# Carrying the routing weight with the slot, adding the other experts' rows while the last expert runs, bringing the last expert's rows to their tokens by a 0/1 product, and spreading the last norm over three engines

## What is computed

```python
# two experts a token, with weights; combine is (token, expert)
weights = jax.nn.softmax(e_top, axis=-1) * g_prob
act = (jax.nn.silu(hg) * hu).astype(jnp.float32) * combine[:, :, None]
y = jnp.einsum('nef,efd->nd', act.astype(x.dtype), w_down)
x = x + gt2[:, None, :] * y
# the final norm
y = xf * lax.rsqrt(jnp.mean(jnp.square(xf), axis=-1, keepdims=True) + EPS)
y = y * gain * (1.0 + scale) + shift
```

## Time and profile before

| | us |
|---|---|
| median of 3 runs | 1399.41 |
| fastest and slowest run | 1393.77, 1399.50 |
| the profiled execution's own time | 1396.18 |
| its span, first to last instruction | 1394.2 |
| PE busy | 1239.2 (89%) |
| PE weight loads busy | 946.7 (68%) |
| DVE busy | 670.4 (48%) |
| ACT busy | 543.9 (39%) |
| POOL busy | 207.4 (15%) |

### The profile page before, as it was taken

How to read it: one execution, slowest core, us unless ns; L and a number is a source line. 1 busy time by engine, 2 the same in 40 slices (tenths; PEclk the granted TensorE clock), 3 DMA queues, 4 the chain that set the end, 5 groups by cost and what they waited for, 6 DMA issues and landing times. The chain is left out here.

```text
span 1394.2 us, 17845 instructions
## 1 busy us (share of the span) xinstructions
PE 1239.2 (89%) x7111; PEld 946.7 (68%) x7111; DVE 670.4 (48%) x900; ACT 543.9 (39%) x872; POOL 207.4 (15%) x237
## 2 busy tenths in 40 slices
PE   3799999999989999998779999999998999999920
PEld 0477876777678887887656566747766888777710
DVE  0516622221151214122466542255686898888846
ACT  2333212101273135214333333302546777777731
POOL 2401300010000010001200011100053222322210
PEclk8699998999999998998889999999999999999965
DMA  9412311244443453438479996821469999999831
GB/s 362 155 61 91 98 35 57 91 161 139 165 158 85 158 206 115 161 121 329 167 252 347 364 352 185 287 86 43 141 229 346 372 369 382 372 375 378 311 145 68
DMA packets 125193, 289.95 MB, mean 208 GB/s; under 512 B 10084, under 2 KB 10204, under 8 KB 120456
## 3 DMA queue, kind: packets, MB, share of 16 engines
q1 hardware_dynamic: 106280, 236.49, 48.0%
q0 software_dynamic: 18848, 52.53, 10.6%
HBM read 270.37 MB, written 26.18 MB: 213 GB/s over the span
## 5 line engine op out<-in xcount | busy, mean ns | idle before, releaser
L962 PE MATMUL psum<-part,part 128*128 128x512 f32 (+1 forms) x1088 | 445.1, 409 | 9.5 <-DVE part L2248 5.9
L963 PE MATMUL psum<-part,part 128*128 128x512 f32 (+1 forms) x1088 | 430.9, 396 | 0.0
L964 PE MATMUL psum<-part,part 128*128 128x512 f32 (+1 forms) x1088 | 430.7, 396 | 0.0
L962 PEld LDWEIGHTS psum<-part,part 128*128 128x128 f32 (+1 forms) x1088 | 228.3, 210 | 76.0 <-issue 24.5
L964 PEld LDWEIGHTS psum<-part,part 128*128 128x128 f32 (+1 forms) x1088 | 228.2, 210 | 40.5
L963 PEld LDWEIGHTS psum<-part,part 128*128 128x128 f32 (+1 forms) x1088 | 229.1, 211 | 35.8
L2248 DVE TENSOR_TENSOR part<-arena,part 128x2048 fp32r<-128x2048 f32 x96 | 218.0, 2290 | 43.3 <-ACT part L1699 41.9
L1803 DVE TENSOR_TENSOR part<-arena,part 128x2048 fp32r<-128x2048 f32 x42 | 96.3, 2299 | 252.5 <-PE psum L1002 228.8
L1699 ACT ACTIVATE part<-arena 128x2048 fp32r<-128x2048 f32 x94 | 178.8, 1919 | 55.8 <-DMA arena<-in_w_up_dram 28.1
L1474 ACT ACTIVATE arena<-psum 128x512 f32<-128x512 f32 (+4 forms) x142 | 77.9, 571 | 272.7 <-PE psum L964 208.9
L950 PE MATMUL psum<-cst,arena 128*128 128x128 f32 (+3 forms) x857 | 128.1, 293 | 61.7 <-DMA cst<-in_consts_dram 12.6
(11 more groups left out here) (271 smaller groups left out, 1073.5 us busy)
## 6 DMA issues: line engine op xcount, KB each, us to landing
arena<-in_w_in_dram SPq DMA_DIRECT2D x34, 1024.0 KB, 5.5
arena<-in_cache_kv_w_dram SPq DMA_DIRECT2D x16, 2048.0 KB, 11.3
arena<-in_w_gate_dram SPq DMA_DIRECT2D x32, 1024.0 KB, 9.7
arena<-in_w_up_dram SPq DMA_DIRECT2D x32, 1024.0 KB, 9.2
arena<-in_w_down_dram SPq DMA_DIRECT2D x32, 1024.0 KB, 10.2
arena<-in_w_ada_dram SPq DMA_DIRECT2D x24, 1024.0 KB, 7.5
arena<-in_cache_kv_w_dram SPq DMA_DIRECT2D x16, 1024.0 KB, 9.0
arena<-in_w_ada_final_dram SPq DMA_DIRECT2D x8, 1024.0 KB, 7.9
```

Source lines behind the costliest of these rows:

```text
L962: nc.tensor.matmul(out_, hi, w_hi, start=start, stop=False)
L963: nc.tensor.matmul(out_, hi, w_lo, start=False, stop=False)
L964: last_product[0] = nc.tensor.matmul(out_, lo, w_hi, start=False, stop=stop)
```

## The change

1. A slot has three words instead of two: token, place, and the weight as float32. DVE computes the weights before it signals `rows_done`, and writes them into the third word of `tok_u`.
2. ACT's `result` uses the third word of `dest_u` as scale, so it waits for `dest_in`, the landing of the places. The weighting after the loop goes away.
3. `yd` is filled with zeros early: a memset and nine transfers on POOL between the two groups of `add_shift`. POOL waits for them before the expert loop, and DVE before it reuses the memory of the zeros.
4. The last expert has no scatter. POOL loads its places, waits for the scatter of the expert before, and loads `yd` back into `yg`, which now lies in the places of weights that have been read. POOL adds the two rows of tiles 2 to 4, DVE those of tiles 0 and 1.
5. DVE builds `hot_last`, ones where a slot's token is the row's, from the last expert's tokens, and PE multiplies it with the last expert's rows (`y_last`, already multiplied by the gate, for the prompt; the plain rows for the sample tile). DVE adds these products from PSUM to `x1`.
6. In the final norm of tiles 0 to 2 ACT scales by the root and POOL adds the shift; DVE does tiles 3 and 4.

```diff
-        slots_d = dram("slots_d", (E_ALL * EROWS + CAP, 2), U32)
+        slots_d = dram("slots_d", (E_ALL * EROWS + CAP, 3), U32)
...
+            nc.gpsimd.memset(zeros, 0.0).then_inc(y_zero, 1)
+            pool.wait_ge(y_zero, 1)
+            for r in range(2 * TOK // P):
+                pool.dma_start(yd[r * P:(r + 1) * P, :], zeros).then_inc(y_zeroed, 16)
...
-            for par in range(2):
-                scatter((E_ALL - 2 + par) * EROWS + (rounds - 1) * CAP, rounds * PAIRS, par)
+            scatter((E_ALL - 2) * EROWS + (rounds - 1) * CAP, rounds * PAIRS, 0)
+            waited()
+            load_places((E_ALL - 1) * EROWS + (rounds - 1) * CAP, 1)
             pool.wait_ge(xg_in[0], rounds * (PAIRS * 16) + 16)
-            for par in range(2):
-                pool.wait_ge(y_out[par], rounds * (PAIRS * 16) + 16)
+            pool.wait_ge(y_out[0], rounds * (PAIRS * 16) + 16)
+            pool.wait_ge(y_out[1], rounds * (PAIRS * 16))
+            pool.wait_ge(gate_filled, rounds * E_ALL)
             waited()
...
+            for i in range(2, TILES):
+                n = ROWS[i]
+                pool.wait_ge(yg_in[i], 16)
+                nc.gpsimd.tensor_tensor(yg[0:n, i, 0, :], yg[0:n, i, 0, :], yg[0:n, i, 1, :], ALU.add).then_inc(y_sum, 1)
...
+                if i < 3:
+                    pool.wait_ge(y_scaled, i + 1)
+                    nc.gpsimd.tensor_tensor(x1[:, i, :], x1[:, i, :], mod[:, 0, 0, :], ALU.add).then_inc(y_shifted, 1)
...
+            for _ in range(2):
+                nc.tensor.matmul(psum[:, 7, :], ident, c_("dmask"), start=True, stop=True)
+            for i in range(TILES):
+                n = ROWS[i]
+                if i == 4:
+                    pe.wait_ge(x2_done, 1)
+                for c in range(2):
+                    if i == 0:
+                        pe.wait_ge(last_done, c + 1)
+                    y = y_last[:, c * CH:(c + 1) * CH] if i < 4 else yb[:, 1, c * CH:(c + 1) * CH]
+                    ins = nc.tensor.matmul(psum[0:n, LAST_BANKS[i][c], :], hot_last[:, i, 0:n], y, start=True, stop=True)
+                ins.then_inc(last_filled, 1)
...
             def result(par, done, after):
                 act.wait_ge(y_out[par], after * 16)
+                act.wait_ge(dest_in[par], after * 16)
                 for c, (filled, out_) in enumerate(((y0_filled, y0_out), (y1_filled, y1_out))):
                     act.wait_ge(filled, done + 1)
-                    nc.scalar.activation(yb[:, par, c * CH:(c + 1) * CH], psum[:, 5 + c, :], ACT.Copy).then_inc(out_, 1)
+                    nc.scalar.activation(yb[:, par, c * CH:(c + 1) * CH], psum[:, 5 + c, :], ACT.Copy,
+                                         scale=dest_w[:, par, :]).then_inc(out_, 1)
...
+            for i in range(TILES):
+                n = ROWS[i]
+                act.wait_ge(x2_done, i + 1)
                 if i:
+                    act.wait_ge(sq3, i)
+                nc.scalar.activation(junk_end[0:n, :], x1[0:n, i, :], ACT.Square, accum_out=ss[0:n, i:i + 1]).then_inc(sq3, 1)
+                act.wait_ge(var3, i + 1)
+                nc.scalar.activation(rs[0:n, i:i + 1], rs[0:n, i:i + 1], ACT.Sqrt).then_inc(sqrt3, 1)
+                if i < 3:
+                    act.wait_ge(rs_done, i + 1)
+                    nc.scalar.activation(x1[:, i, :], yg[:, i, 0, :], ACT.Copy, scale=rs[:, i:i + 1]).then_inc(y_scaled, 1)
...
+            def add_earlier(i):
+                n, s = ROWS[i], i // 4
+                y1, y2, x = yg[0:n, i, 0, :], yg[0:n, i, 1, :], x1[0:n, i, :]
+                if i < 2:
+                    dve.wait_ge(yg_in[i], 16)
+                    own(V.tensor_tensor(y1, y1, y2, ALU.add))
+                else:
+                    dve.wait_ge(y_sum, i - 1)
+                own(V.tensor_tensor(y1, y1, mod[0:n, 2, s, :], ALU.mult))
+                own(V.tensor_tensor(x, x, y1, ALU.add))
...
+            for i in range(2):
+                add_earlier(i)
+            for c, out_ in enumerate((y0_out, y1_out)):
+                cols = slice(c * CH, (c + 1) * CH)
+                dve.wait_ge(out_, rounds * (2 * PAIRS) + 1)
+                V.tensor_tensor(y_last[:, cols], yb[:, 1, cols], mod[:, 2, 0, cols], ALU.mult).then_inc(last_done, 1)
+            add_earlier(2)
+            for i in range(TILES):
+                add_last(i)
+                if i:
+                    last_norm(i - 1)
+                variance(i)
+                if i < 2:
+                    add_earlier(3 + i)
+            last_norm(TILES - 1)
```

More of the change, by code:

```diff
@@ L373, in expert_half @@
             return at(first, 4, CH), *parts(first + HALF, first, 4, CH)
-        yg = at(4 * SLOT, TILES, 2, D)
-        junk_end = at(4 * SLOT + TILES * 2 * D, D)
+        yg = at(0, TILES, 2, D)
+        junk_end = at(TILES * 2 * D, D)
+        hot_last = at(3 * SLOT, TILES, P)
+        y_last = at(3 * SLOT + D, D)
+        zeros = at(KEPT0 + D, D)
         sgubT, sgubTs = stat[:, 640:648], stat[:, 648:656]
@@ L895, in fetch, with load_places @@
                     ap=slot_u[:, par, 0:1], axis=0), bounds_check=TOK - 1, oob_is_err=False).then_inc(xg_in[par], 16)
+            def load_places(row, par):
+                pool.dma_start(dest_u[:, par, :], slots_d[bass.ds(row, CAP), :]).then_inc(dest_in[par], 16)
             def scatter(row, after, par):
-                pool.dma_start(dest_u[:, par, :], slots_d[bass.ds(row, CAP), :]).then_inc(dest_in[par], 16)
+                load_places(row, par)
                 pool.wait_ge(dest_in[par], after * 16)
@@ L2266, in _ @@
                 own(V.tensor_reduce(rowf[:, k, :], pick, AX.X, ALU.add))
+            dve.wait_ge(rt_exp, 2)
+            own(V.tensor_reduce(gp, eg, AX.X, ALU.add))
+            own(V.reciprocal(gp, gp))
+            own(V.tensor_scalar(w1, w2, 1.0, None, ALU.add))
+            own(V.reciprocal(w1, w1))
+            own(V.tensor_tensor(w1, w1, gp, ALU.mult))
+            own(V.tensor_copy(tok_w[:, 0, :], w1))
+            own(V.tensor_tensor(tok_w[:, 1, :], w2, w1, ALU.mult))
             V.tensor_copy(row_u, rowf).then_inc(rows_done, 1)
@@ L2322, in _ @@
             scale_gain(1)
-            def add_experts(i):
-                n, s = ROWS[i], i // 4
-                y1, y2 = yg[0:n, i, 0, :], yg[0:n, i, 1, :]
-                x = x1[0:n, i, :]
-                dve.wait_ge(y1_scaled, i + 1)
-                own(V.scalar_tensor_tensor(out=y1, in0=y2, scalar=w2[0:n, i:i + 1], in1=y1, op0=ALU.mult, op1=ALU.add))
-                own(V.tensor_tensor(y1, y1, mod[0:n, 2, s, :], ALU.mult))
-                V.tensor_tensor(x, x, y1, ALU.add).then_inc(x2_done, 1)
-                dve.wait_ge(x2_done, i + 1)
-                own(V.tensor_tensor(y1, x, mod[0:n, 1, s, :], ALU.mult))
+            own(V.tensor_copy(last_tok, slot_u[:, 1, 0:1]))
@@ new lines, in _ @@
+            for i in range(TILES):
+                ins = V.tensor_scalar(hot_last[:, i, :], c_("iota"), float(P * i), last_tok, ALU.add, ALU.is_equal)
+            own(ins)
+            def add_earlier(i):
+                n, s = ROWS[i], i // 4
+                y1, y2, x = yg[0:n, i, 0, :], yg[0:n, i, 1, :], x1[0:n, i, :]
+                if i < 2:
+                    dve.wait_ge(yg_in[i], 16)
+                    own(V.tensor_tensor(y1, y1, y2, ALU.add))
+                else:
+                    dve.wait_ge(y_sum, i - 1)
+                own(V.tensor_tensor(y1, y1, mod[0:n, 2, s, :], ALU.mult))
+                own(V.tensor_tensor(x, x, y1, ALU.add))
@@ new lines, in add_last @@
+            def add_last(i):
+                n, s = ROWS[i], i // 4
+                dve.wait_ge(last_filled, i + 1)
+                for c in range(2):
+                    cols = slice(c * CH, (c + 1) * CH)
+                    u, x, t = psum[0:n, LAST_BANKS[i][c], :], x1[0:n, i, cols], yg[0:n, i, 1, cols]
+                    if i == 4:
+                        own(V.tensor_tensor(t, u, mod[0:n, 2, 1, cols], ALU.mult))
+                    ins = V.tensor_tensor(x, x, u if i < 4 else t, ALU.add)
+                    if c == 0:
+                        own(ins)
+                ins.then_inc(x2_done, 1)
+                dve.wait_ge(x2_done, i + 1)
+                own(V.tensor_tensor(yg[0:n, i, 0, :], x1[0:n, i, :], mod[0:n, 1, s, :], ALU.mult))
@@ L2343, in _ @@
-            for i in range(TILES + 1):
-                if i < TILES:
-                    add_experts(i)
+                V.reciprocal(rs[0:n, i:i + 1], rs[0:n, i:i + 1]).then_inc(rs_done, 1)
+                if i >= 3:
+                    dve.wait_ge(rs_done, i + 1)
+                    V.scalar_tensor_tensor(out=x1[0:n, i, :], in0=yg[0:n, i, 0, :], scalar=rs[0:n, i:i + 1],
+                                           in1=mod[0:n, 0, s, :], op0=ALU.mult, op1=ALU.add).then_inc(y_done, 1)
+            for i in range(2):
+                add_earlier(i)
```

74 lines of the change are left out of this document (29 added, 45 removed).

## The result

| us | before | after |
|---|---|---|
| median, of 4 runs each | 1399.22 | 1415.75 |
| lowest and highest run | 1393.77, 1399.50 | 1412.51, 1416.90 |
| ratio of the times, with 95% interval | | 1.0125 (1.0098 to 1.0151) |
| profiled execution | 1396.18 | 1416.11 |
| its span | 1394.2 | 1414.4 |

Of the 20.4 us between the two last DVE ops, 17.6 are there at the end of expert 1's result. The positions in time tell the rest: +2.1 from end(1) to end(13), -1.2 over the last two experts, +1.9 in the tail.

The account below looks back on a forecast made before the run. In the expert loop PE was busy 18.00 of 18.00 us and DMA too, at 375 GB/s. Profiled 1396.18 + 19 (wait) + 5 (ring) + 1 (tail) = 1421.2, said as 1421; bounds 1405 to 1433, range 1404 to 1434.

Parts of the forecast that it names:

- D: The prediction's own forecast for the whole kernel: slower, 1405 to 1433 us, chance 0.65.
- The wait on ACT: Expert 0's result waits for its places, PE goes idle, expert 1's result ends later: +19.0 us (bounds +16 and +20).
- steps in series: From expert 0's result to expert 1's, token copies, weight parts, gate, transposes, down products and evictions follow one another: 20.2 us.
- The ring: POOL's loop of scatter, index load, gather and places now includes ACT: period 18.8 us, +5 (bounds 0 and +12).
- The last two experts: End of the expert loop: no fetch in front, down weights set the pace as before, 0 us.
- The tail: From last result to last DVE op: +45.5 us against +44.4, so +1 (bounds -7 and +5).
- The walk: Step-by-step account of DVE's work behind the last result, tile by tile, ending at +46 to +47 us.
- PE's products for tile 0 end before: In the tail, PE's products (0.9 us each after idle) are done before DVE needs them.
- What was free: Zeroing yd early under idle time (13 us if uncovered), moved weight computation (at worst 1.5), third slot word: 0.
- A: Rival at expert 0's result: the wait is hidden and the tail gains; 1389 to 1392 us, chance 0.07.
- B: Rival: the wait is there, but the loop makes the stall good and the tail gains 7; 1401 to 1405 us, chance 0.13.
- C: Rival: POOL's ring bounds at full price and POOL's additions come last in the tail; 1436 to 1445 us, chance 0.15.

Follow-up runs that it names:

- x1: Kernel before plus one line: ACT's result also waits for the landing of the places, nothing else of the change; 1413.50 us, ratio 1.0079.
- x2: Changed kernel with expert 0's places loaded ahead of the modulation loads and each next expert's ahead of the scatter; 1401.37 us, ratio 1.0008.
- x3: Changed kernel with the early additions of tiles 2 to 4 on DVE instead of POOL; 1412.75 us, ratio 1.0084.
- x4: Changed kernel with the last norm step of tiles 0 to 2 back on DVE, without ACT's copy and POOL's addition; 1412.22 us, ratio 1.0078.
- x6: x5 with the six loads of the final modulation (2.25 MB) moved behind the scatter of expert 14; 1397.99 us, ratio 1.0000 to the kernel before.
- x7: Kernel before with only the six final modulation loads (2.25 MB) moved behind the scatter of expert 14; 1390.92 us, ratio 0.9938.
- x5: Changed kernel with the edits of x2, x3 and x4 together; 1393.99 us, ratio 0.9974 to the kernel before.
- x8: x5 with an expert's result behind the token copies and first two high parts in ACT's order; 1394.65 us, ratio 0.9976 to the kernel before.
- x9: x8 with modulation loads split by need: gate behind expert 14's scatter, scale and shift behind yd tiles 1 and 2; 1384.45 us, ratio 0.9911 to before.

## Why the prediction was right, point by point

The forecast D held: 1421 was said, 1415.75 measured (profiled 1416.11), slower by more than the measurement's error. The change itself came out smaller than said: the terms add up to 25 us, and the profiled executions are 19.9 apart, the medians 16.5. The two largest terms were both too large.

1. **The wait on ACT** (+19, bounds 16 to 20). Right in mechanism and nearly in size. First result at 1076.7 for 1078, end(0) 1078.0 for 1079.1, PE idle to 1083.13 for 1083, end(1) 1097.9 for 1099.3. The steps in series took 19.9 us for 20.2. The term measured +17.6, of which 1.6 came with the entry into the expert part; the remaining 16.0 are at the low bound. x1 shows it by itself, x2 takes most of it away. The places landed faster than the 5.3 us of my choice: the first landing is some 4 us behind its issue at 1072.46, as DMA was running out of work (226 GB/s from 1072 to 1077, after 313 in the five us before), with the weights stopped by the same stall. The landings of L914 in the changed kernel:

```profile
DMA to landing us min/median/max: 3.5/6.1/7.2
```

2. **The ring** (+5). This is the term that was mis-sized: +2.1. Its signs came, with 11 of 13 results right behind their places, but the period was 18.54 and not 18.8. The scatter took 1.01 in nearly every turn and not 1.2, the gather 1.05 to 2.6 and not 2.4, the places 5.65 in the turn shown and not 6.2. In a ring each small term counts once a turn: 0.26 us too much, twelve times, is 3 us. I had taken durations from single turns. That the ring costs anything over the loop isn't shown: from end(1) to end(13) the kernels in which ACT waits for places in most turns take 221.1 (x1), 222.3 (x3), 222.5 (after) and 223.4 us (x4), those in which it waits once or twice or never 220.1 (x6), 220.4 (before), 220.7 (x7), 220.9 (x2) and 223.2 (x5).

3. **The last two experts** (0). They gave 1.2 us back: 35.33 us from end(13) to end(15) against 36.54. The cause of that wasn't tried; x1 to x7 lie between 35.4 and 36.9, so it may be chance.

4. **The tail** (+1, bounds -7 to +5). +1.9 in the one profile, +1.0 by the means of three tails each (45.5 and 44.5). The walk was right in its places: DVE at the first tile at -4.4, `y_last` done at +10.6 for +11.7, tile steps of 5.3, 8.9, 5.2, 5.2 and 7.8 us for 5.5, 9.3, 5.5, 5.5 and 7.9. Added up, the walk gave +46 to +47, and 46.3 came; the +45.5 that went into the sum was lower than the walk, for no reason that a row gives. One step failed inside it: "PE's products for tile 0 end before". The earlier trace rows counts records, and a product of this kind leaves two: L1286 makes 32 full products in the kernel before and has 64 records. The changed kernel's chain:

```profile
1365.72 3.79 PE psum L1491 x4
```

These four records are the two products of tile 0. After 9.03 us of idle they take 1.9 us each, not 0.9, and end 0.95 us too late for DVE. DVE also waits 2.25 us in each of three tiles for ACT's square, which stands behind its copy. x4 has these three waits no more, for three operations of 1.28 us on DVE; its wait for PE stays (0.89).

5. **What was free.** Zeroing `yd` was, as said. POOL's timeline of the changed kernel:

```profile
68.30 0.95 POOL L799 MEMSET arena<- 128x1024 f32 x1
69.54 4.77 POOL L802 DMA_DIRECT2D yd<-arena  x9 [0.30 <-POOL arena L799]
130.62 2.88 POOL L794 TENSOR_TENSOR arena<-arena 128x1024 f32<-128x1024 f32 x1 [56.31 <-DVE arena L1933]
```

56.31 us of idle are left behind it.

6. **The rivals.** A (the wait hidden) fell with the first line of ACT's timeline: the condition was places landed before 1063, and they landed near 1076.5. B (the stall made good) was wrong in both halves: end(15) - G is 16.9 longer, as much as end(1) - G (16.0), so nothing was made good, and of the tail's 7 us most (6.1) came only in x5, with POOL out of it. C (the ring at full price) didn't come: the period stayed at 18.54. The range's low end, 1404, was 8.5 us below the fastest run; the high end, 1434, would have needed gathers of 3.0 us each turn and a tail 5 us longer.

What stays open: why the loops of x2, x5 and x8 are 5 to 6 us longer than before's although the places now come before the scatter. Part of it may be the fast execution of before, since x2's ratio is only 1.0008. The late first result (end(0) - G is 32.3 in x2 and x5, 27.2 before) isn't enough as a cause: x6 has it too (32.7), and with the modulation loads moved its loop is 307.8; x8 has no wait for places on ACT and still takes 314.2. So the runs point at the modulation loads, which x2, x5 and x8 also start some 4 us later than before. x9 changes ACT's order and the loads at once, so their shares aren't told apart.

## What to carry to other kernels

When a value travels with a table that an engine didn't have to read before, look up in the trace when that table lands now, and lay it beside the time at which its new reader wants it: a slack of a whole stage on a side engine costs nothing until something in the middle waits for it. Ask what stands ahead of the small load in its own queue: moving big transfers there that nobody needed yet made the kernel before 0.6% faster (x7), and gained nothing in x6, where their new place made the tail wait. Before giving additions to GpSimd, look at what VectorE runs beside them: where both read SBUF the sum of the two can be longer than VectorE alone.

## What the runs showed of the hardware that was not expected

- A load of 1.5 KB into 128 rows took 2.9 to 3.5 us at the least, where DMA was running out of work, 6.1 in the median beside weights at 370 GB/s, and some 12 to 15 behind 2.25 MB in its own queue (12.42 to 14.97 us of POOL idle in nine kernels; 4.18 in x7, 5.61 in x6, 5.80 in x9, which have moved the 2.25 MB).
- A float32 product of 128 x 512 leaves two records: 0.47 us each without idle before (the filler products, 1.88 us for four), 0.95 each after 9 us of idle. PE's timeline of the changed kernel:

```profile
1354.82 1.88 PE L1482 MATMUL psum<-cst 128*128 128x512 f32 x4
1365.72 6.51 PE L1491 MATMUL psum<-arena 128*128 128x512 f32 x8 [9.03 <-DVE arena L2413]
```

- The two filler products ahead of `last_filled` ended 9 us before the products they stand in front of. The first products behind the idle time then ran at half the fillers' rate. The stretch between them, its granted clock 0.75 on average (from 2.4 towards 1.2 GHz), busy times in the order given above:

```profile
1356.70:1365.70 9.00, 0.00 (x0) 0.00 (x0) 8.93 (x4) 0.00 (x0) 7.48 (x3) 0.75 0.16 35
```
- ACT's emptying of 128 x 512 from PSUM takes 0.68 us with a scale for each row and 0.60 without: 0.16 us a turn, inside the ring.
